# The next stream's row norm moved into the feed-forward stage, half of its transposes ahead of the last down projection

## The reference

```python
for l in range(DEPTH):
    h = modulate(rms_norm(x, norm1[l]), sh1, sc1)
    hc = modulate(rms_norm(ctx, norm1[l]), csh1, csc1)
    ... = jnp.split(h @ w_in[l], IN_SPLITS, axis=-1)
    ...
    x = x + g1 * branch_merge(ya, yb, ga, gb, w_pa[l], w_pb[l], w_o[l])
    if not last:
        ctx = ctx + cg1 * branch_merge(ya_c, yb_c, gac, gbc, w_pa[l], w_pb[l], w_o[l])
    h2 = modulate(rms_norm(x, norm2[l]), sh2, sc2)
    x = x + g2 * swiglu_2(h2, w_ffn_in[l], w_ffn_out[l])
    ...
```

## Time and profile before

| | |
|---|---|
| median of 3 runs | 2001.18 us |
| lowest, highest | 1998.55, 2005.02 us |
| the profiled execution | 2001.95 us, span of its instructions 2000.2 us |
| mean granted clock of PE | 0.98 |
| PE busy | 1887.6 us, 94% |
| POOL busy | 1357.9 us, 68% |
| ACT busy | 928.3 us, 46% |
| DVE busy | 732.3 us, 37% |

### The profile page before, as it was taken

One profiled execution on the slowest core, in us unless ns is written; L12 is line 12 of the kernel. 1 busy time (PEld: TensorE's weight loads), 2 busy tenths in 40 slices (PEclk: granted clock), 3 DMA queues, 4 the chain that ended last, 5 costly groups with the idle time before them and its releaser, 6 DMA issues.

```text
span 2000.2 us, 28307 instructions
## 1 busy us (share of the span) xinstructions
PE 1887.6 (94%) x9582; PEld 1498.9 (75%) x9582; DVE 732.3 (37%) x1291; ACT 928.3 (46%) x1458; POOL 1357.9 (68%) x780
## 2 busy tenths in 40 slices
PE   7987999889899999999999999999999999999997
PEld 5666788676678878677888787778887787778885
DVE  1375433357421126345111445452113545451112
ACT  5454534343454344565434445644444445644442
POOL 5504999450498877666988784478886784478883
PEclk9998999989999999999999999999999999999999
DMA  7757566547765554434775452246754452245551
GB/s 259 232 191 263 180 196 195 181 154 259 237 223 190 183 184 130 149 122 129 216 207 186 145 168 93 90 145 179 213 185 147 148 158 96 95 137 179 188 184 69
DMA packets 257208, 344.32 MB, mean 172 GB/s; under 512 B 33376, under 2 KB 153056, under 8 KB 257120
## 3 DMA queue, kind: packets, MB, share of 16 engines
q1 hardware_dynamic: 243328, 337.13, 52.6%
q10 hardware_dynamic: 13792, 6.03, 1.8%
HBM read 342.03 MB, written 1.05 MB: 172 GB/s over the span
## 4 chain that ended last, share of the span: by engine, by line
PE 86%; DVE 6%; ACT 3%; DMA 2%; issue 2%; POOL 1%; SPq 0%; ACTq 0%; DVEq 0%
PE bank L1971 24%; PE bank L1973 24%; PE bank L1972 24%; PE bank L2042 3%; PE bank L2512 2%; PE bank L2502 2%; PE bank L2529 2%; PE bank L2021 1%; ACT wh L663 1%; PE bank L2053 1%; PE bank L2208 1%; PE bank L2288 1%; DVE xl L1181 1%; DMA raw<-in_l_w_in 1%; DVE xh L1179 1%
## 5 line engine op out<-in xcount | busy, mean ns | idle before, releaser
L642 POOL TENSOR_TENSOR wl<-raw,wh 128x1024 fp32r<-128x1024 f32 x300 | 731.5, 2451 | 89.7 <-ACT wh L801 83.5
L1971 PE MATMUL bank<-wh,xh 128*128 128x512 f32 (+2 forms) x1746 | 693.5, 397 | 32.3 <-issue 11.2
L627 POOL TENSOR_TENSOR wl<-raw,wh 128x512 fp32r<-128x512 f32 (+2 forms) x238 | 321.4, 1350 | 525.9 <-ACT wh L663 497.4
L1973 PE MATMUL bank<-wl,xh 128*128 128x512 f32 (+2 forms) x1746 | 676.3, 387 | 0.0
L1972 PE MATMUL bank<-wh,xl 128*128 128x512 f32 (+2 forms) x1746 | 675.0, 387 | 0.0
L801 ACT ACTIVATE wh<-raw 128x1024 fp32r<-128x1024 f32 x270 | 286.5, 1062 | 445.2 <-PE bank L1973 431.7
L1971 PEld LDWEIGHTS bank<-wh,xh 128*128 128x128 f32 x1746 | 330.9, 190 | 109.0 <-issue 34.2
L1973 PEld LDWEIGHTS bank<-wl,xh 128*128 128x128 f32 x1746 | 330.8, 189 | 67.3
L1972 PEld LDWEIGHTS bank<-wh,xl 128*128 128x128 f32 x1746 | 331.7, 190 | 62.5 <-issue 1.4
L663 ACT ACTIVATE wh<-raw 128x1024 fp32r<-128x1024 f32 (+2 forms) x268 | 274.2, 1047 | 210.1 <-PE bank L1973 149.5
L628 POOL TENSOR_TENSOR wl<-raw,wh 128x512 fp32r<-128x512 f32 (+2 forms) x238 | 321.1, 1349 | 0.0
(11 more groups left out here) (316 smaller groups left out, 1674.1 us busy)
## 6 DMA issues: line engine op xcount, KB each, us to landing
raw<-in_w_ffn_in SPq DMA_DIRECT2D x264, 256.0 KB, 3.0
raw<-in_w_in SPq DMA_DIRECT2D x224, 256.0 KB, 2.9
raw<-in_w_mod SPq DMA_DIRECT2D x192, 256.0 KB, 3.7
raw<-in_w_ffn_out SPq DMA_DIRECT2D x132, 256.0 KB, 2.9
raw<-in_l_w_gate SPq DMA_DIRECT2D x88, 256.0 KB, 3.6
raw<-in_l_w_up SPq DMA_DIRECT2D x88, 256.0 KB, 4.4
raw<-in_l_w_down SPq DMA_DIRECT2D x88, 256.0 KB, 2.9
raw<-in_l_w_in SPq DMA_DIRECT2D x48, 256.0 KB, 4.4
```

Source lines behind the costliest of these rows:

```text
L627: nc.gpsimd.tensor_tensor(wl[:, s, 0:h], raw[:, s, 0:h], words(wh)[:, s, 0:h], ALU.subtract)
L642: nc.gpsimd.tensor_tensor(wl[:, s, :], raw[:, s, :], words(wh)[:, s, :], ALU.subtract)\
L1971: mm(dst, x_hi, w_hi, start=first, stop=False, skip_group_check=True)
L1973: return mm(dst, x_hi, w_lo, start=False, stop=last, skip_group_check=True)
```

## The change

`mix_c0`, `mix_x0` and `mix_c1` are moved as follows. ACT's `norm_roots` is done in the feed-forward stage ahead of it, after its loop and before the conversion of chunks 64 and 65 (`ahead`). DVE's `norm_scale` and `norm_rows` are done there too, before the last step's product (DVE's loop is one step shorter, and that step stands behind it). PE does the first two of the four pairs of transposes between the last hidden transposes and the last down projection, the other two after it. `norm_turned` and `norm_splits` stay where they are in the order of ACT and DVE. For `mix_x1` PE does the first two pairs between the two chunks of c1's tile 2, the other two where all four stood. POOL waits, at the third chunk of `in_c0`, `in_x0`, `in_c1` and the fourth of `in_x1`, until two pairs of the norm are split.

```diff
@@ POOL
+                    norm = {"in_c0": "mix_c0", "in_x0": "mix_x0", "in_c1": "mix_c1", "in_x1": "mix_x1"}.get(name)
                     for j in range(j0, plan.end(name)):
+                        if norm and j == j0 + (3 if name == "in_x1" else 2):
+                            pool.wait_ge(xt_split, split_at[norm] + 2)
                         if j not in plan.whole:
                             lo(j, size(j))
@@ ACT, ffn(name, sg, pieces=(), ahead=lambda: None)
                 at[0] = j1 + (FF_STEPS - 2) * RING
+                ahead()
                 hi_until(j0 + FF_CH)
...
-            ffn("ffn1", sg1)
+            ffn("ffn1", sg1, ahead=lambda: norm_roots("mix_c0", C, lambda t: act.wait_ge(ctx_in, 16)))
...
-                    mod_norm(f"mix_{name}", s, l, 0, ready)
+                    act.wait_ge(scale_set, norm_no[f"mix_{name}"] - 3)
+                    norm_turned(f"mix_{name}", lambda k: nscale[:, k:k + 1], lambda k: mod_col(l, 0, k, s))
...
-            half_block(CTX, 0, lambda t: act.wait_ge(ctx_in, 16))
-            half_block(XS, 0, lambda t: residual_done("ffn1", t))
-            half_block(CTX, 1, lambda t: residual_done("ffn_c0", t))
+            half_block(CTX, 0, lambda: norm_roots("mix_x0", X, lambda t: residual_done("ffn1", t)))
+            half_block(XS, 0, lambda: norm_roots("mix_c1", C, lambda t: residual_done("ffn_c0", t)))
+            half_block(CTX, 1)
@@ DVE, ffn(name, sg, h, meanwhile=None, ahead=None)
-                with dve.Fori(0, FF_STEPS - 1) as i:
+                with dve.Fori(0, FF_STEPS - 2) as i:
                     hidden(gub, i)
+                if ahead:
+                    ahead()
+                hidden(gub, FF_STEPS - 2)
...
+            def early_norm(s, l):
+                norm_scale(s, l, 1)
+                norm_rows(f"mix_{'cx'[s]}{l}", (C, X)[s])
...
                 if name != "x1":
-                    norm_scale(s, l, 1)
-                    row_norm(f"mix_{name}", (C, X)[s])
+                    norm_splits(f"mix_{name}")
...
-            add = half_block(CTX, 0, lambda: post_ffn("ffn1"))
-            add = half_block(XS, 0, add)
+            ffn("ffn1", sg1, h1, ahead=lambda: early_norm(CTX, 0))
+            add = half_block(CTX, 0, lambda: post_ffn("ffn1"), lambda: early_norm(XS, 0))
+            add = half_block(XS, 0, add, lambda: early_norm(CTX, 1))
@@ PE, rows_turn(name, pairs=range(4)) and ffn(name, h, between, ahead=None)
-                for pair in range(KD // 2):
+                for pair in pairs:
...
+                if ahead:
+                    rows_turn(ahead, (0, 1))
                 down(j0 + FF_CH - DN_CH, step=FF_STEPS - 1, last=True)
...
-                rows_turn(f"mix_{name}")
+                rows_turn(f"mix_{name}", (2, 3))
...
                 if name == "c1":
-                    gemm("in_c1", x_name="mix_c1")
+                    for i in range(3):
+                        if i == 1:
+                            pe.wait_ge(res_done, TT * (res_no[AHEAD["mix_c1"]] + 1))
+                        if i < 2:
+                            column_tile("in_c1", i, 0, "mix_c1" if i == 0 else None)
+                    pe.wait_ge(evac, plan.tile_no["in_c1"])
+                    tile_chunk("in_c1", 2, 0)
+                    rows_turn("mix_x1", (0, 1))
+                    tile_chunk("in_c1", 2, 1)
```

More of the change, by code:

```diff
@@ L779, in residual_done, with ffn @@
                 act.wait_ge(res_done, TT * res_no[name] + t + 1)
-            def ffn(name, sg, pieces=()):
+            def ffn(name, sg, pieces=(), ahead=lambda: None):
                 f, j0 = FFNS.index(name), plan.first[name]
@@ L1072, in evac_in, with half_block @@
                 nc.scalar.activation(gsd, gsq, ACT.Sqrt, scale=1.0 / HD, bias=eps6).then_inc(g_std, 1)
-            def half_block(s, l, ready=None):
+            def half_block(s, l, ahead=lambda: None):
                 name = f"{'cx'[s]}{l}"
@@ L1145, in half_block @@
                 ffn(f"ffn_{name}", sg2, [lambda h=h: load_bias(("c0", "x0").index(name), (h, h + 1)) for h in range(0, NAH, 2)]
-                    if name != "x1" else [])
+                    if name != "x1" else [], ahead)
                 tail(f"ffn_{name}")
-            half_block(CTX, 0, lambda t: act.wait_ge(ctx_in, 16))
-            half_block(XS, 0, lambda t: residual_done("ffn1", t))
-            half_block(CTX, 1, lambda t: residual_done("ffn_c0", t))
+            half_block(CTX, 0, lambda: norm_roots("mix_x0", X, lambda t: residual_done("ffn1", t)))
+            half_block(XS, 0, lambda: norm_roots("mix_c1", C, lambda t: residual_done("ffn_c0", t)))
+            half_block(CTX, 1)
             half_block(XS, 1)
@@ L1252, in post_ffn, with ffn @@
                 post_add(name)
-            def ffn(name, sg, h, meanwhile=None):
+            def ffn(name, sg, h, meanwhile=None, ahead=None):
                 f = FFNS.index(name)
@@ L1807, in head_norm, with half_block @@
                 v.engine_nop().then_inc(qkv_ready, 1)
-            def half_block(s, l, last_addition=lambda: None):
+            def early_norm(s, l):
+                norm_scale(s, l, 1)
+                norm_rows(f"mix_{'cx'[s]}{l}", (C, X)[s])
+            def half_block(s, l, last_addition=lambda: None, ahead=None):
                 name = f"{'cx'[s]}{l}"
@@ L1945, in half_block @@
                 row_norm(f"ffn_{name}", dst)
-                ffn(f"ffn_{name}", sg2, h2)
+                ffn(f"ffn_{name}", sg2, h2, ahead=ahead)
                 return lambda: gated_ffn(f"ffn_{name}", dst)
-            add = half_block(CTX, 0, lambda: post_ffn("ffn1"))
-            add = half_block(XS, 0, add)
+            ffn("ffn1", sg1, h1, ahead=lambda: early_norm(CTX, 0))
+            add = half_block(CTX, 0, lambda: post_ffn("ffn1"), lambda: early_norm(XS, 0))
+            add = half_block(XS, 0, add, lambda: early_norm(CTX, 1))
             half_block(CTX, 1, add)
@@ L2043, in turn, with rows_turn @@
                 ins.then_inc(done, 1)
-            def rows_turn(name):
+            def rows_turn(name, pairs=range(4)):
                 n = norm_no[name]
@@ L2063, in rows_turn, with ffn @@
                     turn(turn_banks(name)[pair], lambda i, t: rows[:, t, (2 * pair + i) * P:(2 * pair + i + 1) * P], norm_tr)
-            def ffn(name, h, between=lambda: None):
+            def ffn(name, h, between=lambda: None, ahead=None):
                 f, j0 = FFNS.index(name), plan.first[name]
@@ L2421, in _ @@
             rows_turn("ffn1")
-            ffn("ffn1", h1, lambda: mod_turn(1))
+            ffn("ffn1", h1, lambda: mod_turn(1), "mix_c0")
             def gate_rows(name):
@@ L2582, in half_block @@
                 rows_turn(f"ffn_{name}")
-                ffn(f"ffn_{name}", h2)
+                ffn(f"ffn_{name}", h2, ahead={"c0": "mix_x0", "x0": "mix_c1"}.get(name))
             half_block(CTX, 0)
```

1 line of the change is left out of this document (removed).

## The result

The changed kernel took a median of 1991.3 us (six runs, 1991.01 to 1994.71) beside 2001.88 us for the kernel before on the same chip (six runs). The ratio of the two is 0.9936, with a 95% interval of 0.9908 to 0.9963: faster, by 10.6 us. The profiled execution took 1991.01 us, its span is 1989.1 (before 2001.95 and 2000.2). The forecast was 1991.6.

What follows compares the result with a forecast made beforehand. PE, busy 94% of the span, was taken as the bound, so gains come from its waits and slow stretches: x0 4.7, c0 5.2, c1 and x1 0.5, in sum 10.4 us off 2001.95, giving 1991.6; range 1984 to 1998.

Steps and rivals of the forecast that it cites:

- x0, 4.7 forecast: Start of x0: stop of 4.01 us shrinks to 0.95 and a slow stretch of 1.7 goes; 4.7 us taken.
- c0, 5.2 forecast: c0: 5.5 us gained if the squares are not held again, less 0.3 for POOL's delay by DVE.
- the wait of 1.08 us: PE's wait for POOL in c0 at 786.78, laid to DVE's 9.27 us squares; forecast to go.
- a rarity (two in 60): Of some 60 stretched DVE instructions, all but two were held for one POOL instruction; so c0's squares would not be again.
- c1 and x1, 0.5 forecast: c1 and x1 as one chain: 2.2 us gained less a 1.7 us slow stretch; ends -0.5 and 7.4.
- the term 2.2 us: x1: last split at 1580.5 against 1582.71 before, so only 2.2 us earlier, with DVE's casts held by POOL.
- Held again in c0: Rival, chance 0.24: c0's squares meet unbroken POOL work again; c0 gives 0.8 us, total 1996.0.
- Splits of x1 unheld: Rival, chance 0.14: POOL's hold reaches x1's casts; x1 gives 7.4 less 0 to 2 us, total 1985.
- The slow stretches are not the wait's: Rival, chance 0.12: slow stretches in x0, c0, c1 only shift with the work; gain 7 us, total 1995.
- Slower: Rival, chance 0.05: residual's last addition on DVE held 8.5 us longer in c0 or x0; one hold 2002, two 2012.
- POOL's hold, costed at nothing: POOL holds its third next chunk 3.3 us later, for a chunk PE wants 10 us after that: no cost.
- The early norm and its table loads: Feed-forward stage: ACT's roots and table loads, DVE's row scalings lie under 10.9 us of PE products: no cost, uncovered up to 5.

Runs made afterwards that it cites:

- e2: Changed kernel with all four transpose pairs of mix_c0, mix_x0, mix_c1 after the last down projection, POOL's hold in x1 only; 1999.93 us, ratio 0.9997.
- e3: Changed kernel with the norm's roots and row scalings back behind the last Silu and last hidden step, transposes still early; 2013.86 us, ratio 1.0043.
- e4: Changed kernel with PE waiting for all four split pairs, instead of two, ahead of tile 0 of c0, x0 and c1; 1999.34 us, ratio 0.9987.
- e5: Kernel before with only the change's c1 and x1 part (early transposes for x1, POOL's hold in x1); 1999.15 us, ratio 0.9998.
- e6: Kernel before with one added POOL wait in c0 until DVE has its sums of squares; 2000.98 us, ratio 0.9992.
- e9: Changed kernel with one more c1 chunk rounded early on ACT and the third context turn behind x1's second tile; 1985.63 us, again 1987.65.
- e1: Changed kernel without POOL's hold (its wait for two split pairs); 1991.62 us, ratio 0.9948.
- e8: Changed kernel with the third context turn (c1's keys) moved behind x1's second tile instead of the first; 1991.31 us, ratio 0.9943.
- e7: Changed kernel with ACT rounding one more weight chunk of c1 before the roots of x1's norm; 1992.9 us, ratio 0.9947.

## Why the prediction came out right

**The time** (1991.6 forecast, 1991.3 and 1989.07 measured). The mechanism was the one forecast, and e2, e3 and e4 show its three conditions one by one: transposes early, norm in time, tile 0 content with two pairs. Without any one of them the interval of the ratio to the kernel before takes in 1 (e2, e4) or lies above it (e3). What was luck in the fit of the sum stands further down.

**x0, 4.7 forecast, 4.8 in the profiles.** No wait at tile 1: the residual ended at 1138.1 on DVE and PE came at 1139.01. The margin forecast as 0.8 us was 0.9. What I gave as one sum is 3.2 us that came in every profile and 1.6 that the kernel before paid in x0 in one of its two profiles (three of the six with such a stop).

**c0, 5.2 forecast, 5.8 in the profiles.** The wait of about 0.5 us at tile 1 came (0.47), the squares were held by one instruction only, and the wait of 1.08 us went. The mis-sized term is what the wait of 1.08 us was worth: about 1.2 less 0.3 in the sum, 1.6 in the traces, since the pace behind it was slower too. But the reason given for the squares, that a hold over seven POOL instructions is a rarity (two in 60), was only half right: it came in both profiles of the kernel before, and in none of the twelve others. Here is the changed kernel's timeline of DVE, then POOL's, at that place:

```profile
766.40 1.12 DVE L1767 TENSOR_TENSOR arena<-arena 128x640 f32<-128x640 f32 x1
```

```profile
765.53 1.30 POOL L628 TENSOR_TENSOR wl<-raw,wh 128x512 fp32r<-128x512 f32 x1
766.78 1.89 POOL L627 TENSOR_TENSOR wl<-raw,wh 128x512 fp32r<-128x512 f32 x1
```

What decides it is open. In the two profiles of the kernel before the squares start 0.18 and 0.19 us after a POOL instruction does (POOL's timeline in the first and the second):

```profile
770.13 1.29 POOL L628 TENSOR_TENSOR wl<-raw,wh 128x512 fp32r<-128x512 f32 x1
```

```profile
778.61 1.30 POOL L628 TENSOR_TENSOR wl<-raw,wh 128x512 fp32r<-128x512 f32 x1
```

In e5 and e6, with the same c0 but for the slow stretch, they start 1.07 and 1.09 us after one and take 0.91. In e2, with the same slow stretch in c0 and at almost the same moment (770.34), they start 0.08 us after one and take 1.89 us. That the phase decides is argued, not shown.

**c1 and x1, 0.5 forecast, 1.7 in the profiles (0.9 + 0.9).** Each step came as told: a wait of about 2.3 us at c1's tile 1 (2.09), a wait of over 4 us at the third turn (4.52), and a slow stretch behind it (1.6 us; forecast 1.7). What was mis-sized is the term 2.2 us, by which the third turn was to come earlier: it came 3.3 us earlier. To compare it with the forecast, which counts from an unchanged start of c1, the 8.0 us that c0 and x0 had won by then must be added to the times of the changed kernel. The last split ended at 1571.94, which is 1580.0 so counted, against 1580.5 forecast and 1582.71 before: 2.7 us earlier. The first cast came 1.4 us later than forecast, behind the slow stretch in c1 that I had not counted, but DVE lost less by holds: three instructions took 2.59, 1.66 and 1.51 us, 4.2 us more than unheld, where I had five holds of 1.25. The other 0.6 us is that in the kernel before the turn came 0.6 us after the copies of the keys were done (it waited for ACT), and now comes right behind them.

That the splits set the turn, e4 shows. From the end of the last split to the turn 11.2 to 11.3 us go by in all eight profiles with x1's early transposes that leave the turn behind tile 0. In e4 the splits came 3.4 us earlier, counted from c1's first product, and so did the turn (47.3 us instead of 50.7). DVE's last split in the changed kernel, then DVE's and PE's rows in e4:

```profile
1571.25 0.69 DVE L1186 TENSOR_TENSOR xl<-xf,xh 128x512 fp32r<-128x512 f32 x1
```

```profile
1578.41 0.70 DVE L1186 TENSOR_TENSOR xl<-xf,xh 128x512 fp32r<-128x512 f32 x1
```

```profile
1590.32 0.44 PE L2052 MATMUL bank<-con,xf 128*128 128x128 f32 x2 [4.39 <-DVEq L1813]
```

**What c1 earned** I had at nothing of its own, and it was 0.9: the 3.2 us of the stop less the wait of 2.09 us. The slow stretch did not go, it moved from behind the stop to behind the wait; I had counted that wait without one.

**The rivals.** *Held again in c0*: no, with L1767 at 1.12 us. *Splits of x1 unheld*: no, three of the eight were held, and the last ended 2.7 us earlier and not 7.4. *The slow stretches are not the wait's*: they are the wait's (none of 21 places without it), but not of every wait. My reading of the waits of 3.3 us, once none and once most of 6.74 us, left out the third of them in the same trace, 3.32 us at 1346.14 with 5.44 us of small products behind it. *Slower*, by an addition held on DVE: no such hold in any profile of the change; but see below for one of 16.56 us elsewhere.

**POOL's hold, costed at nothing,** was worth nothing in c0, x0 and c1 and 1.1 us less than nothing in x1. **The early norm and its table loads, at nothing,** lie where forecast: ACT at 723.6 to 727.8 us, DVE at 726.5 to 728.8, some 10 us ahead of the transposes.

**What was not forecast** is in the rest: 3.31 us of wait for the row norm of ffn_c0 had no slow stretch behind it in the first profile of before (32 small products in 4.05 us) and had one in both profiles of the changed kernel, 2.3 us. Nothing shows that the change brings it: the second profile of before has 1.3 us of it, e5, e6 and the second of e9 have none.

```profile
932.48 6.69 PE L2063 MATMUL bank<-rdiag,extra 128*128 128x128 f32 x32 [3.31 <-DVE rdiag L1196]
...
1784.21 5.52 PE L2063 MATMUL bank<-rdiag,X 128*128 128x128 f32 x32 [3.31 <-DVE rdiag L1196]
```

The second line is ffn_x1, where it went the other way by 1.2 us. Together they took back 1.1 us, against some 2 us by which c0, x0, c1 and x1 gave more than forecast. The close fit of the sum is in part this, and so luck. It is luck too that the one profile from which I took the two slow stretches of c0 and x0 had both.

**The rule weighed.** The Trainium skill, "SBUF — State Buffer", section "SBUF: two separate sides", has whoever starts first keep the port pair for the whole instruction. The changed kernel's squares go by it (DVE at 1.12, POOL behind it at 1.89). The trace disagrees where it costs most: the squares' 9.27 us lie over seven POOL instructions, in both profiles of the kernel before, and end only 0.7 us after the last of them.

## What to carry to other kernels

A stop between two stages of a matmul engine is the latency of the first operand through transposes, eviction and split, and half of the operand made during the last products of the stage before removes it, provided that the norm is ready then and that the first tile asks for only that half. Behind each stop that goes, look for the next thing by stage: here it was a weight chunk that ACT reached too late and a turn that could stand one tile later, and moving both gave another 5 to 6 us of stage time. Count a slow clock behind a stop at what share of the executions have it, and take such small parts from matching stages of two traces, since the rest of the kernel moves by several us from run to run.

## What the runs showed of the hardware

**A DVE instruction can be held beside POOL for far longer than one instruction.** The second profile of the kernel before took 2009.93 us, 8 more than the first. Its lag behind the first grows at one place, from 1.2 to 11.5 us, and later stretches give 3.5 back. At that place a DVE multiplication that takes 2.52 us in the first profile of before took 16.56, beside seven POOL instructions without a gap, and PE waited 8.71 us for what followed. Timelines of DVE, POOL (the first of the eight ended before the multiplication began) and PE:

```profile
223.56 16.56 DVE L1362 TENSOR_TENSOR arena<-arena,small 128x1024 f32<-128x1024 f32 x1
```

```profile
220.27 18.77 POOL L642 TENSOR_TENSOR wl<-raw,wh 128x1024 fp32r<-128x1024 f32 x8
```

```profile
241.97 1.11 PE L2042 MATMUL bank<-con,arena 128*128 128x128 f32 x4 [8.71 <-DVE arena L1263]
```

In the fourteen profiles of this study a DVE instruction of over 6.5 us occurs three times: this one and the squares twice.

**The clock fell after waits of 2.1 us** at c1's tile 1 (mean granted clock 0.56 over 3.9 us, and as slow in all four profiles with that wait), and did not fall after some stops of 4.0 us, in which PE had done 1 to 1.9 us of transposes at the start. A shorter wait is no safeguard: in the attention of c0 PE waits 1.45 us twice in every profile, and in five of the fourteen (e1, e3, e6, e8 and the second of e9) 3.4 us at a granted clock of 0.50 follow one of them. In x1 it fell after a stop of 3.2 us with 2.18 us of waiting in e5, and did not after one of 3.2 us with 2.11 in e2, nor after stops of 3.5 us with 2.5 in e7 and the first profile of e9. Which of the places with a stop get it differs between executions of one kernel (x0 in the two profiles of before); in the two profiles of the changed kernel the places are the same.
